# Two-layer diffusion step: sixteen modulation items read later, the convolution's first transforms in halves, another opening order

## The reference

```
mod   = silu(cond) @ mod_w + mod_b            # shift, scale, gate, twice
h     = rms_norm(x) * (1 + sc1) + sh1
proj  = h @ w_in                              # Hyena | q k v | short conv | gates
ya    = order-2 Hyena: twice z = part * fftconv(z, filter_o)
yb    = attention with rotary;  yc = gated 3-tap convolution
x    += g1 * ((sum of sigmoid(gate_b) * (y_b @ w_br_b)) @ w_o)
h2    = rms_norm(x) * (1 + sc2) + sh2
x    += g2 * expert_choice_moe(h2)            # 16 experts, top 16 and top 64 tokens each
```

## Time and profile before

| | |
|---|---|
| median of three runs | 2371.03 us |
| profiled execution | 2374.17 us |
| its span, first to last instruction | 2372.5 us |
| mean granted TensorE clock | 0.964 |
| TensorE matmuls busy | 2204.2 us, 93% |
| VectorE busy | 1389.1 us, 59% |
| ScalarE busy | 998.8 us, 42% |
| DMA | 436.19 MB, mean 184 GB/s |

### The profile page before, as it was taken

How to read it: one execution, slowest core, us unless ns; L and a number is a source line. 1 busy time by engine, 2 the same in 40 slices (tenths; PEclk the granted TensorE clock), 3 DMA queues, 4 the chain that set the end, 5 groups by cost and what they waited for, 6 DMA issues and landing times.

```text
span 2372.5 us, 38587 instructions
## 1 busy us (share of the span) xinstructions
PE 2204.2 (93%) x14538; PEld 1859.6 (78%) x14538; DVE 1389.1 (59%) x2253; ACT 998.8 (42%) x1780; POOL 167.9 (7%) x221
## 2 busy tenths in 40 slices
PE   7998999999888998699997999999897999599999
PEld 3447999999645996588886999999763898388887
DVE  4756533611766654788887443431358764688887
ACT  2333222222631223588885321222360222488885
POOL 0000000010100100111110000001100110011110
PEclk8999999999999998799998999999998999799999
DMA  9792222233324431899992222233401341599995
GB/s 367 281 335 80 76 85 72 110 119 116 131 114 159 161 103 65 317 383 388 382 389 80 72 78 83 81 122 120 166 22 44 126 136 54 210 387 388 384 377 190
DMA packets 72959, 436.19 MB, mean 184 GB/s; under 512 B 9289, under 2 KB 9929, under 8 KB 31930
## 3 DMA queue, kind: packets, MB, share of 16 engines
q1 hardware_dynamic: 46368, 331.89, 36.5%
q0 software_dynamic: 21728, 86.51, 11.3%
q10 hardware_dynamic: 4732, 16.00, 1.9%
HBM read 384.87 MB, written 49.50 MB: 183 GB/s over the span
## 4 chain that ended last, share of the span: by engine, by line
PE 83%; DVE 8%; ACT 3%; issue 2%; DMA 2%; DVEq 2%; ACTq 0%; POOLq 0%
PE ps L610 39%; PE ps L1046 8%; PE ps L1076 7%; PE ps L1034 5%; PE ps L1050 4%; PE ps L785 4%; PE ps L907 2%; PE ps L704 2%; PE ps L835 1%; PE ps L644 1%; PE ps L921 1%; PE ps L924 1%; PE ps L686 1%; PE ps L992 1%; DVE nb L1816 1%
## 5 line engine op out<-in xcount | busy, mean ns | idle before, releaser
L610 PE MATMUL ps<-front_r 128*128 128x320 f32 x5888 | 934.8, 312 | 27.8 <-DVE front_r L1545 13.5
L610 PEld LDWEIGHTS ps<-front_r 128*128 128x128 f32 x5888 | 885.4, 189 | 34.7 <-issue 13.8
L1529 DVE TENSOR_TENSOR front_r<-ring,front_r 128x1024 fp32r<-128x1024 f32 x148 | 181.1, 1224 | 474.1 <-ACT front_r L1141 472.9
L1141 ACT ACTIVATE front_r<-ring 128x1024 fp32r<-128x1024 f32 (+1 forms) x180 | 176.4, 980 | 375.1 <-PE ps L610 291.8
L1141 ACT ACTIVATE back<-ps 128x480 f32<-128x480 f32 (+5 forms) x240 | 113.1, 496 | 423.6 <-PE ps L610 165.7
L1046 PE MATMUL ps<-back_r 128*80 128x256 f32 x640 | 171.8, 291 | 0.0
L1046 PE MATMUL ps<-back_r,front_r 128*80 128x256 f32 x640 | 164.2, 279 | 0.0
L1984 DVE TENSOR_TENSOR back_r<-front,back_r 128x512 fp32r<-128x512 f32 x208 | 137.8, 688 | 26.8 <-ACT back_r L1141 23.4
L1076 PE MATMUL ps<-back_r,front_r 128*80 128x512 f32 x576 | 149.6, 395 | 0.0
L610 PE MATMUL ps<-back_r,front_r 128*128 128x320 f32 x640 | 148.1, 313 | 0.0
L1141 ACT ACTIVATE back_r<-front 128x512 fp32r<-128x512 f32 x208 | 126.3, 637 | 12.5 <-PE ps L1050 6.5
(11 more groups left out here) (240 smaller groups left out, 3145.7 us busy)
## 6 DMA issues: line engine op xcount, KB each, us to landing
ring<-in_stream SPq DMA_DIRECT2D x186, 1024.0 KB, 7.7
front<-in_stream SPq DMA_DIRECT2D x80, 1024.0 KB, 13.5
back<-in_stream SPq DMA_DIRECT2D x48, 1024.0 KB, 14.6
gates<-back POOLq DMA_DIRECT2D x48, 320.0 KB, 2.4
back<-gates POOLq DMA_DIRECT2D x48, 320.0 KB, 3.3
kspec<-back POOLq DMA_DIRECT2D x20, 512.0 KB, 7.3
front<-kspec POOLq DMA_DIRECT2D x4, 2048.0 KB, 11.6
rows<-front ACTq DMA_DIRECT2D x10, 520.0 KB, 3.3
```

What stands on the lines that cost most here:

```text
L610: mm = pe.matmul(tokh(b)[:, c0:c1], w(wp)[:, k, :], src(hp, k)[:, c0:c1], start=first, stop=last)
L1141: return act.activation(o, i, ACT.Copy)
L1529: dve.tensor_tensor(half_dst(u, 1), src, half_dst(u, 0).bitcast(F32), ALU.subtract).then_inc(w_lo, 1)
```

## The change

The kernel computes the same. **Stream order:** 32 modulation items are read in the opening, four in layer 0's convolution (two per order), eight at layer 0's choice of tokens and four at layer 1's; the items at a choice stand right before the experts' items. **Opening:** SyncE holds back item 1 and all later ones until the network's input has landed; only items 0 to 2 are used before the steps, steps 0 to 2 and 14 to 19 have two items, the others one; `cft` and the second decay are loaded by POOL's queue, after X and before the constants; `magnitude` is done in four halves, and a window waits for its own. **Convolution:** the first half of the frequencies is transformed in two pieces of 256 channels (`forward_first`), the second in one (`forward_second`); VectorE does sums and products per piece (`products`, four multiplications as before) and the combination once (`combine`, the six operations as before); the semaphores count one more step each. **Choice:** TensorE does the items after the token tiles, the last one after the places; ScalarE copies and adds them after it has stored the rows; the experts' items are issued in the order 0, 1, 2, 4, 5, 3, 6 and so on. **keep_busy:** matmuls of 256 columns, whose result nothing reads, around `mean_squares` and `spread`: 4 and 6 in layer 1's first norm, 5, 1 and 4 in each layer's second.

The diff, cut to its added and removed lines (the new `products` and `combine`, which hold the old multiplications and additions, are left out):

```diff
@@ -64,18 +64,25 @@
-MODS, LATE = DEPTH * N_MOD, 12
-EARLY = MODS - LATE
+MODS, LATE = DEPTH * N_MOD, (4, 8, 4)
+EARLY = MODS - sum(LATE)
...
-    return EARLY + l * ITEMS + p + (LATE if l or p >= P_BR else 0)
+    late = sum(LATE[:2 * l] if l else LATE[:int(p >= P_BR)])
+    return EARLY + l * ITEMS + p + late + (LATE[1 + l] if p >= P_EXP else 0)
...
-    return i if i < EARLY else EARLY + P_BR + i - EARLY
+    if i < EARLY:
+        return i
+    if i < EARLY + LATE[0]:
+        return place(0, P_BR) - LATE[0] + i - EARLY
+    if i < MODS - LATE[2]:
+        return place(0, P_EXP) - (MODS - LATE[2]) + i
+    return place(1, P_EXP) - MODS + i
@@ -93,7 +100,7 @@
-        x = (g - MODS) % ITEMS - P_EXP if g >= MODS + P_BR else -1
+        x = g - place(int(g >= place(1, 0)), P_EXP)
@@ -322,11 +329,20 @@
-            return mrow[:, i % 4, :] if i < EARLY else late_row[:, i % 2, :]
+            return late_row[:, i % 2, :] if EARLY <= i < EARLY + LATE[0] else mrow[:, i % 4, :]
...
-            return (6 + n,) if n < 10 else (2 * n - 4, 2 * n - 3)
+            if n < 3:
+                return 3 + 2 * n, 4 + 2 * n
+            return (6 + n,) if n < 14 else (2 * n - 8, 2 * n - 7)
+        def conv_mods(o):
+            return range(EARLY + LATE[0] // 2 * o, EARLY + LATE[0] // 2 * (o + 1))
+        def choice_mods(l):
+            first = EARLY + sum(LATE[:l + 1])
+            return range(first, first + LATE[l + 1])
@@ -456,8 +472,12 @@
+                    if g == 1:
+                        sp.wait_ge(lay_net, 32)
...
-                for x in range(LAP):
+                for x in (0, 1, 2, 4, 5, 3, *range(6, LAP)):
@@ -486,6 +506,9 @@
+            for i in range(2):
+                pool.dma_start(cft[:, i], a["cft"][:, i]).then_inc(cft_in, 16)
+            pool.dma_start(dec[1], a["decay"][1]).then_inc(dec_in, 16)
@@ -631,6 +654,11 @@
+            def keep_busy(bank, n):
+                for _ in range(n):
+                    pe.matmul(ps[:, bank, 0:2 * P], ident[:], csi[:].rearrange("p r n -> p (r n)"), start=True, stop=True)
@@ -717,9 +745,8 @@
-            for i in range(2, 6):
-                modulation(i)
-                warm(1)
+            modulation(2)
+            warm(1)
@@ -747,7 +774,9 @@
+                    keep_busy(1, 4)
...
+                    keep_busy(1, 6)
@@ -896,15 +925,28 @@
-                    def forward(kt):
+                    def wait_tokens(odd):
+                        if o:
+                            pe.wait_ge(y_out, l * 5 + 2 + 3 * odd)
+                    def forward_first(half):
+                        c0 = 256 * half
...
-                            if o and kt == 0:
-                                pe.wait_ge(y_out, l * 5 + 2 + 3 * odd)
+                            if half == 0:
+                                wait_tokens(odd)
...
-                                    mm = pe.matmul(ps[:, 4 * kt + 2 * odd + r, :], CSF[:, r, 2 * odd + t, P * kt:P * kt + P],
+                                    mm = pe.matmul(ps[:, 2 * half + odd, 256 * r:256 * r + 256],
+                                                   CSF[:, r, 2 * odd + t, 0:P],
+                                                   u_tm[:, 1 + 2 * odd + t, c0:c0 + 256], start=t == 0, stop=t == 1)
+                        mm.then_inc(y_fwd, 1)
+                    def forward_second():
+                        for odd in range(2):
+                            for r in range(2):
+                                for t in range(2):
+                                    mm = pe.matmul(ps[:, 4 + 2 * odd + r, :], CSF[:, r, 2 * odd + t, P:2 * P],
@@ -928,19 +970,19 @@
-                    forward(0)
+                    forward_first(0)
+                    forward_first(1)
...
-                        pe.wait_ge(modcol_read, EARLY + LATE // 2)
-                    forward(1)
+                        pe.wait_ge(modcol_read, conv_mods(0)[-1] + 1)
+                    forward_second()
...
-                        pe.wait_ge(y_odd, 2 * o + 2)
-                        i0 = EARLY + LATE // 2 * o
-                        for i in range(i0, i0 + LATE // 2):
+                        pe.wait_ge(y_odd, 3 * o + 3)
+                        for i in conv_mods(o):
...
-                            if i > i0:
+                            if i > conv_mods(o)[0]:
...
-                        mod_columns(i0 + LATE // 2 - 1)
+                        mod_columns(conv_mods(o)[-1])
@@ -981,8 +1023,13 @@
+                pe.wait_ge(mg_read, l * MG + 24 + 5)
+                keep_busy(1, 5)
...
+                keep_busy(1, 1)
...
+                keep_busy(1, 4)
@@ -1011,9 +1058,18 @@
+                for i in choice_mods(l)[:-1]:
+                    mod_rows(i)
+                    if i > choice_mods(l)[0]:
+                        mod_columns(i - 1)
+                mod_columns(choice_mods(l)[-2])
...
+                mod_rows(choice_mods(l)[-1])
+                mod_columns(choice_mods(l)[-1])
@@ -1102,6 +1158,8 @@
+                pe.wait_ge(modcol_read, choice_mods(l)[-1] + 1)
@@ -1201,6 +1259,8 @@
+                if t == 0:
+                    act.wait_ge(f_dec, n // 5 + 1)
@@ -1218,22 +1278,15 @@
-            for i in range(1, 5):
-                mod_copy(i)
+            mod_copy(1)
+            mod_copy(2)
...
-            mod_copy(5)
-            for i in range(2):
-                act.dma_start(cft[:, i], a["cft"][:, i]).then_inc(cft_in, 16)
-            act.dma_start(dec[1], a["decay"][1]).then_inc(dec_in, 16)
...
-            act.wait_ge(f_dec, 1)
...
-                if n == 9:
-                    act.wait_ge(f_dec, 2)
@@ -1376,20 +1429,23 @@
-                for n in range(4):
-                    o, kt = n // 2, n % 2
-                    act.wait_ge(y_fwd, l * 6 + 3 * o + kt + 1)
+                for o in range(2):
...
-                        act.wait_ge(y_sum, l * 4 + n - 1)
-                    copy(yodd[kt], ps[:, 4 * kt + 2:4 * kt + 4, :]).then_inc(y_odd, 1)
-                    if l == 0 and kt:
-                        i0 = EARLY + LATE // 2 * o
-                        for i in range(i0, i0 + LATE // 2):
+                        act.wait_ge(y_sum, l * 4 + 1)
+                    for half in range(2):
+                        act.wait_ge(y_fwd, l * 8 + 4 * o + half + 1)
+                        copy(yodd[0].rearrange("p r n -> p (r n)")[:, DH * half:DH * half + DH],
+                             ps[:, 2 * half + 1, :]).then_inc(y_odd, 1)
+                    act.wait_ge(y_fwd, l * 8 + 4 * o + 3)
+                    if o:
+                        act.wait_ge(y_sum, l * 4 + 2)
+                    copy(yodd[1], ps[:, 6:8, :]).then_inc(y_odd, 1)
+                    if l == 0:
+                        for i in conv_mods(o):
...
-                            if i > i0:
+                            if i > conv_mods(o)[0]:
...
-                        late_add(i0 + LATE // 2 - 1)
+                        late_add(conv_mods(o)[-1])
@@ -1439,6 +1495,11 @@
+                for i in choice_mods(l):
+                    mod_copy(i)
+                    if i > choice_mods(l)[0]:
+                        late_add(i - 1)
+                late_add(choice_mods(l)[-1])
@@ -1645,9 +1706,9 @@
-            def magnitude(l):
-                dve.scalar_tensor_tensor(out=dec[l], in0=dec[l], scalar=-1.0, in1=dec[l], op0=ALU.mult,
-                                         op1=ALU.max).then_inc(f_dec, 1)
+            def magnitude(l, o):
+                d = dec[l][:, :, o, :]
+                dve.scalar_tensor_tensor(out=d, in0=d, scalar=-1.0, in1=d, op0=ALU.mult, op1=ALU.max).then_inc(f_dec, 1)
@@ -1655,17 +1716,20 @@
-            magnitude(0)
-            for i in range(1, 5):
-                mod_add(i)
+            magnitude(0, 0)
+            mod_add(1)
...
-                if n == 8:
+                if n == 1:
+                    magnitude(0, 1)
+                elif n == 8:
...
-                    magnitude(1)
+                    magnitude(1, 0)
+                elif n == 9:
+                    magnitude(1, 1)
@@ -1867,8 +1928,32 @@
+                    for half in range(2):
+                        c0, c1 = 256 * half, 256 * half + 256
+                        settle()
+                        dve.wait_ge(y_odd, l * 6 + 3 * o + half + 1)
+                        even = ps[:, 2 * half, :].rearrange("p (r n) -> p r n", r=2)
+                        odd = yodd[0].rearrange("p r n -> p (r n)")[:, DH * half:DH * half + DH]\
+                            .rearrange("p (r n) -> p r n", r=2)
+                        dve.tensor_tensor(ysum[:, 0, :, c0:c1], even, odd, ALU.add)
+                        ins = dve.tensor_tensor(ysum[:, 1, :, c0:c1], even, odd, ALU.subtract)
+                        if half:
+                            ins.then_inc(y_sum, 1)
+                        settle()
+                        products(0, c0, c1)
+                    combine(0)
...
-                    dve.wait_ge(y_fwd, l * 6 + 3 * o + 3)
```

(9 more changed lines are left out.)

15 lines of the change are left out of this document (5 added, 10 removed).

## The result

The changed kernel takes **2359.05 us** (median of 5 runs, 2356.69 to 2361.47) against 2375.78 for the kernel before (now 5 runs, 2369.81 to 2377.66): ratio **0.993**, 95% interval 0.9918 to 0.9942, so 16.7 us faster. The forecast was 28.5 us faster, 2342.5, with a range of 2331 to 2354: the sign was right, the size was not, and the time lies outside the range. The profiled execution took 2358.94 us; its span is 2357.2, 15.3 us less than before. Two executions that were far slower than all others (4344.67 us of the kernel before, 7875.69 of `four_groups_opening`) are left out of the ratios.

A forecast was written before the change was run, and what follows sets the result against it. The prediction took the kernel to be TensorE work (83% of the chain) with a few stretches in which TensorE waits. Its seven steps summed to -28.5 us, 2342.5 us on the median, with a range of 2331 to 2354.

The forecast's parts named there:

- Step 6: Layer 0's choice of tokens: eight modulation items there delay the first gather and some expert items, +5.0 us.
- step 5: Keep-busy matmuls around the norms: high clock speeds spread and logits, -7.8 us; cost before layer 1's first norm, +0.7.
- step 4: Convolution by halves: VectorE starts sooner, second order limited by its spectrum's load, -7.0 us over both layers.
- step 2: Opening's new order: bytes bind until step 5 of the filter loop, which starts sooner, -4.7 us.
- Step 1: Opening: four modulation items fewer, -5.5 us; the halved magnitude passes give nothing.
- Step 3: Layer 0's convolution: two landed items per order hide beside VectorE's work, -9.7 us.
- Step 7: Layer 1's choice of tokens: four landed items, one expert item beside the gather, +0.5 us, 0 to +2.
- A: Choice of tokens: the backlog drains ahead of the first experts, +12 us, 2354; chance 0.12.
- B: Warm matmuls don't hold the clock or run cold: 7.8 us lost, up to 2 added, 2351; chance 0.10.
- C: Layer 0's convolution: late items don't hide, 2 x 4.5 us, 2351; chance 0.06.
- E: Experts become DMA-bound, slower at 2378 us; chance 0.04.
- D: Opening held by the chain, not by bytes: 4 us more gained, 2338; chance 0.08.

The follow-up runs named there:

- four_groups_opening: Changed kernel with late items in four groups of four, spectrum in parts, no keep-busy at layer 1's first norm, network's second layer first, second decay after constants: 2338.27 us.
- opening_order_before: Changed kernel with the opening's order of before, still 32 early items: 2357.10 us, ratio 0.992.
- experiment 7: Two opening edits of the changed kernel: network's second layer ahead of modulation item 1, 2356.18 us; the order of before with 32 early items, 2357.10 us.
- experiment 2: Changed kernel with the first transforms of both layers whole again, ScalarE's copies and VectorE's products kept: 2364.82 us, ratio 0.9954.
- experiment 5: Changed kernel with the second order's filter spectrum fetched in three transfers, each as soon as its place is free: 2353.80 us, ratio 0.9907.
- experiment 3: Changed kernel without the keep-busy matmuls around both second norms and layer 1's first: 2362.75 us, ratio 0.9954.
- experiment 4: Two edits of the changed kernel's choice: expert items after the second held for the first gather, 2361.10 us; layer 0's places turned after the fourth item, 2361.33 us.
- network_first: Changed kernel with the filter network's second layer ahead of modulation item 1 on TensorE, its argument ahead of item 0's sum on VectorE: 2356.18 us.

## Why the prediction was wrong, step by step

Of the 28.5 us the two profiles show 15.3. Of the 13.2 that are missing 7.5 lie in the two choices of tokens (steps 5 to 7), 3.6 in the two convolutions (steps 3 and 4), 1.3 in the opening (1 and 2), and 0.8 in the other stages. Step 6 failed by most (the delay of the places and the gather), then step 5 (the size of the gain), step 4 (the wait for the spectrum) and step 2 (the new order).

**Step 1 (-5.5): the cause right, the term too small.** `opening_order_before` has only this step's changes in the opening, four items fewer and the halved magnitude passes: 7.8 us. The four items are 5.5 of it, 1.37 each. Another 1.0 is the step in which the second decay's magnitude was taken: from step 10 to step 11 it took 7.15 us and now takes 4.81, of which 1.37 is the item. The chain of the kernel before has that pass on it:

```profile
85.84 2.28 DVE back L1649
```

The prediction had called the halved passes "beside TensorE: nothing". The whole pass was on the path, and halved it isn't. The last 1.3 us are 0.6 ahead of step 5, within the scatter, and 0.7 behind the last step, where the chain of the kernel before waits for a store of the spectra (7.71 us) and the new one doesn't.

**Step 2 (-4.7): wrong.** It measured 0 within the scatter (experiment 7). That bytes hold the opening to near 60 us was right in kind: the DMA's share is 0.96 to 1.02 from 10 us to there in both orders. But by step 5 not 19.3 MB had moved but 22.3 (371 GB/s over 60.13 us), and 22.6 in the order of before: the sum had too little for what the four ring slots prefetch, and the new order paid with a late item 1 (11.91 us after its issue) and with TensorE idle from 25 to 29.8 us, so that step 0 ran at the low clock: taps in 3.78 us, not 1.72.

**Step 3 (-9.7): right.** With two items the first order takes 19.68 us in layer 0, and without any it takes 19.68 in layer 1.

**Step 4 (-7.0): the first order right, the second not.** In the first order 22.78 became 19.68, 3.1 of the 3.3 forecast. In the second, 22.71 became 23.67 in layer 1. Before:

```profile
1812.62 13.90 PE L907 MATMUL ps<-back,front 128*128 128x512 f32 x32
1835.33 3.40 PE L946 MATMUL ps<-back,csi 128*128 128x512 f32 x4 [8.82 <-DVE back L1856]
```

The new wait was named, but mis-sized: the spectrum took 12.2 us and not 11.6 and was asked for 4.05 us ahead of the forward transform and not 4.5, so VectorE started 8.35 us after that transform began, where it had started after 8.1 before. From there its operations up to the sums need 15.3 us instead of 14.6. That is 0.7 us for the splits. The prediction took 0.5; by the Trainium skill, "VectorE: DVE Perf Modes", section on the TRN2 errata, it had worked out 0.94 per order, and the measured value lies midway. Behind a longer idle gap (9.7 us) TensorE then ran the inverse transforms partly at the low clock, another 1.0. So layer 1 gained 1.4; experiment 2 shows the same first-order gain in layer 0 and none in its second order; and experiment 5, which takes the wait away, gave 3.6 to 4.4 more per layer.

**Step 5 (-7.8 + 0.7): the cause right, the size wrong.** Measured against the changed kernel -1.75, -2.45 and +0.95, and against all runs with this code some -2.9, -2.8 and +1 (experiment 3): half to three quarters of the term. The logits gave 2.4 us per layer of the 2.6 forecast. The spread's 1.2 came in 14 of the 22 spreads behind the second norm, in the eleven runs with five and one keep-busy matmuls there; in the others the granted clock was already 0.50 behind the mean of squares, whose ten matmuls have one column each. And in layer 0 what was gained ahead of the items was partly lost to the DMA behind them.

**Step 6 (+5.0): wrong, and the largest miss.** In the changed kernel the eight items cost 9.6 us in this stage: the places were turned 4.1 us later than they would have been, where the step had 0 within 0 to 2, and the gather took 5.5 us more, not 3.5. With step 5's 3.6 us gained (logits and spread) that is the +6.1 of the table. Without the keep-busy matmuls, when TensorE gets to the items later, they cost 7.8 us (63.15 against 55.34): 2.7 for the places and 4.9 for the gather. What the step left out is TensorE's fall to the low clock in its first wait for an item, after which a cycle takes 2.80 us, and the columns, which wait for ScalarE. The 1.5 us priced for the third and fourth expert items did not come (experts 311.96 us against 312.91). The Trainium skill, "DMA: Bandwidth & Descriptors", section on queues, rings and completion order, would have the gather wait for its turn only; the trace agrees that it isn't last: issued at 945.75 it landed at 955.21, ahead of an item that was issued before it, at 942.81, and landed at 959.31. But the price is well above the 2 us that the prediction had drawn from it: 9.46 us with four items outstanding and a fifth issued just behind, 5.53 with one issued just behind, 4.03 with nothing beside it. And experiment 4 shows what the step had missed altogether: a shorter gather doesn't help, for the experts' items are the next to be late.

**Step 7 (+0.5): too small, within its 0 to +2.** 1.6 (57.14 against 55.54 without keep-busy matmuls).

**The rivals.** A (the backlog drains ahead of the experts) is the one that came true, in part: its +12 would have been for all of it. B, the warm matmuls, came true for 8 of 22 spreads. C, E and F did not happen, D neither: chain and bytes end together. The range failed because its upper end let one rival come true alone, and here the misses of steps 2, 4, 5 and 6 have one sign and added up. Part of them has one cause, which the sum did not join: time that an edit frees ahead of a transfer is partly spent in waiting for it.

## What to carry to other kernels

Work moved into a stretch costs its bytes as well as its cycles. If the stretch behind it lives on a full DMA, reordering queues or a faster wait only moves the loss; taking megabytes out returned it here. Look for a place where both the engine and the DMA are idle, as layer 1's convolution was, and where the data isn't needed sooner. When an edit makes a stage's first half faster, ask which transfer is issued by that stage's own progress: it doesn't get shorter. Read an edit of a few us in its stage, over several runs, since stages that it doesn't touch differ by 2 to 4 us from run to run.

## What the runs showed of the hardware

Idle time of TensorE is often paid twice. After gaps of 5.7 to 10.3 us the context's four records took 3.4 to 3.8 us in every run; in the ten second orders of the experiments that filled it, 1.96 to 1.99. There useful items filled it as well as matmuls that do nothing, and the gain is only as large as what TensorE has on the path afterwards (1.4 us of 3.8). But a filled gap is no guarantee. In the first orders with two items, where TensorE idles only 1.1, 0.6 and 0.6 us at a time, the same code gave both clocks, here the changed kernel and then `network_first`:

```profile
684.38 3.57 PE L988 MATMUL ps<-back,csi 128*128 128x512 f32 x4
```

```profile
681.92 1.98 PE L988 MATMUL ps<-back,csi 128*128 128x512 f32 x4
```

It cost nothing there, since VectorE is what the next step waits for. And with the same code layer 1's inverse transforms took 10.5 to 11.8 us. Why one run kept the clock and the next lost it stays open.

A 1 MB item in the ring took 7.4 us to land in the median, but 18.1 and 19.1 us where many transfers were outstanding: the DMA was busy for the whole of both waits (share 1.02 and 1.00, 365 and 418 GB/s).
